# A two-layer decoder trunk on one core: raw transposes of the memory, new x's squares behind two high parts, interleaved attention heads, down's end by bank

## What is computed

```python
mem_n = rmsnorm(mem, mem_norm)                 # 256 memory tokens
for layer in range(2):
    h = rmsnorm(x, g[0])
    mix = even_mixer(h, ...) if layer % 2 == 0 else odd_mixer(h, ...)
    x = x + rmsnorm(mix, g[1])
    h = rmsnorm(x, g[2])
    x = x + rmsnorm(memory_cross_attention(h, mem_n, wq, wk, wv, wo), g[3])
    h = rmsnorm(x, g[4])
    x = x + rmsnorm((silu(h @ w_gate) * (h @ w_up)) @ w_down, g[5])
# memory_cross_attention: q = h @ wq, k = mem_n @ wk, v = mem_n @ wv, 4 heads of 512,
# p = softmax(q k^T / sqrt(512)), o = p v, o @ wo
```

## Time and profile before

| | before |
|---|---|
| median of 3 runs | 3000.12 us (2994.8 to 3000.22) |
| profiled execution, its own time | 2996.18 us |
| its span | 2994.4 us |
| mean granted TensorE clock | 0.984 of 2.4 GHz |
| VectorE busy | 2139.9 us (71%) |
| ScalarE busy | 1543.4 us (52%) |
| high part of a chunk, ScalarE, x550 | 1.914 us each |
| low part of a chunk, VectorE, x550 | 2.290 us each |
| squares of a token tile, ScalarE, x12 | 1.922 us each |
| `x_update`, VectorE, x10 | 2.346 us each |

### The profile page before, as it was taken

How to read it: one execution, slowest core, us unless ns; L and a number is a source line. 1 busy time by engine, 2 the same in 40 slices (tenths; PEclk the granted TensorE clock), 3 DMA queues, 4 the chain that set the end, 5 groups by cost and what they waited for, 6 DMA issues and landing times. The chain is left out here.

```text
span 2994.4 us, 31754 instructions
## 1 busy us (share of the span) xinstructions
PE 2890.6 (97%) x13082; PEld 2392.7 (80%) x13082; DVE 2139.9 (71%) x1443; ACT 1543.4 (52%) x1363; POOL 47.0 (2%) x97
## 2 busy tenths in 40 slices
PE   7999999999999999999998999999999999999998
PEld 6888788787787888887887877787787888887886
DVE  7888778568468988884456768567558888886454
ACT  5666556445345655664444445435435666555442
POOL 0000000000000000000000000000000000000000
PEclk9999999999999999999999989999999999999999
DMA  7664754655456455656554615644554655566552
GB/s 267 225 260 178 283 175 167 218 180 214 144 177 223 178 183 204 225 221 228 196 188 135 228 57 208 231 169 155 197 183 169 225 202 183 181 222 253 191 190 83
DMA packets 238272, 583.44 MB, mean 195 GB/s; under 512 B 8752, under 2 KB 8768, under 8 KB 222640
## 3 DMA queue, kind: packets, MB, share of 16 engines
q1 hardware_dynamic: 232896, 530.61, 49.8%
q0 software_dynamic: 4064, 38.21, 3.3%
q10 hardware_dynamic: 1168, 12.59, 1.0%
HBM read 564.60 MB, written 16.78 MB: 194 GB/s over the span
## 5 line engine op out<-in xcount | busy, mean ns | idle before, releaser
L1054 DVE TENSOR_TENSOR w_lo<-wide,w_hi 128x2048 fp32r<-128x2048 f32 x550 | 1250.9, 2290 | 490.9 <-ACT w_hi L554 487.8
L554 ACT ACTIVATE w_hi<-wide 128x2048 fp32r<-128x2048 f32 x550 | 1048.0, 1914 | 491.1 <-PE ps L1691 389.7
L1691 PE MATMUL ps<-w_hi,act_hi 128*128 128x512 f32 x3332 | 1227.8, 392 | 27.2 <-DVE w_lo L1054 11.5
L1691 PE MATMUL ps<-w_lo,act_hi 128*128 128x512 f32 x3332 | 1222.5, 391 | 0.0
L1691 PE MATMUL ps<-w_hi,act_lo 128*128 128x512 f32 x3332 | 1222.3, 391 | 0.0
L1691 PEld LDWEIGHTS ps<-w_hi,act_hi 128*128 128x128 f32 x3332 | 628.4, 189 | 163.1 <-issue 13.7
L1691 PEld LDWEIGHTS ps<-w_hi,act_lo 128*128 128x128 f32 x3332 | 628.8, 189 | 131.5
L1691 PEld LDWEIGHTS ps<-w_lo,act_hi 128*128 128x128 f32 x3332 | 629.1, 189 | 130.2 <-issue 0.2
L1058 DVE TENSOR_TENSOR wide<-wide,wide 128x2048 f32<-128x2048 f32 x105 | 240.5, 2290 | 4.8
L1691 PE MATMUL ps<-w_hi,s_hi_kept 128*128 128x512 f32 x368 | 149.0, 405 | 19.1 <-DVE nat L1615 13.6
L1009 ACT ACTIVATE act_hi<-mid 128x256 fp32r<-128x256 f32 x80 | 33.7, 421 | 240.4 <-PE ps L1691 240.4
(11 more groups left out here) (244 smaller groups left out, 1681.1 us busy)
## 6 DMA issues: line engine op xcount, KB each, us to landing
wide<-in_ffn_w_gate SPq DMA_DIRECT2D x88, 1024.0 KB, 7.7
wide<-in_ffn_w_up SPq DMA_DIRECT2D x88, 1024.0 KB, 7.1
wide<-in_ffn_w_down SPq DMA_DIRECT2D x88, 1024.0 KB, 4.9
wide<-in_odd_w_in SPq DMA_DIRECT2D x48, 1024.0 KB, 5.4
wide<-in_xattn_wk SPq DMA_DIRECT2D x32, 1024.0 KB, 8.2
wide<-in_xattn_wv SPq DMA_DIRECT2D x32, 1024.0 KB, 7.4
wide<-in_even_w_in SPq DMA_DIRECT2D x32, 1024.0 KB, 7.1
wide<-in_xattn_wq SPq DMA_DIRECT2D x32, 1024.0 KB, 5.2
```

What stands on the lines that cost most here:

```text
L554: nc.scalar.activation(w_hi[:, c % W_SLOTS, :], src, ACT.Copy).then_inc(hi_done, 2)
L1054: nc.vector.tensor_tensor(w_lo[:, c % W_SLOTS, :], src, w_hi[:, c % W_SLOTS, :].bitcast(F32), ALU.subtract).then_inc(lo_done, 2)
L1691: return nc.tensor.matmul(dst, lhs, rhs, start=start, stop=stop, skip_group_check=loose)
```

## The change

- The memory is transposed raw, its first half loaded in four quarters at the head of SP's queue, the second between chunks 1 and 2. The gain is the scale of the evacuations (`round_mem`, `rest_mem`), the root the scale of the keys' and values' evacuations. ScalarE's queue carries the vector rows first, now with `mem_norm`, and `x` after the second rounding. The squares of `x` lie in the second strip of the first keys, its `normed` in the value strips, its first transposes before the last product of the second layer's values.
- Behind a norm VectorE updates both halves of x at once, and takes the roots after the second low part and the first sums. ScalarE makes two high parts before it squares both halves.
- Attention goes head by head: scores, transposes and weighted values interleaved; the weighted values use banks 0 to 3; the next product waits for single banks.
- Down: the last `mid` transposes come before the fourth row; at the end one row is done for the first tile before the last three are waited for, one after another.

```diff
-    def stage(name, seven=(), rounds=0, rows=0, taken=True):
+    def stage(name, seven=(), rounds=0, rows=0, taken=True, uses=0):
...
+        at["u"] += uses
...
-        stage(f"x_pv{l}", rounds=2)
+        stage(f"x_pv{l}", uses=2)
...
-        return 4 + 4 * (TURNS.index(pre) + 1)
+        return 2 if pre == "mem_norm" else 4 + 4 * (TURNS.index(pre) + 1)
...
-        pxt = px
+        pxt = place("pxt", [XH, MT, T], F32, area + 16 * KB)
...
+        mem_in = [sem(f"mem_in{b}") for b in range(4)] + [sem("mem_in_other")]
+        pv_done = sem("pv_done")
...
+                if n == 2:
+                    sp.dma_start(memx[:, 1, :], mem[P:2 * P, :]).then_inc(mem_in[4], 16)
...
+            for b in range(4):
+                cols = slice(b * NB, (b + 1) * NB)
+                sp.dma_start(memx[:, 0, cols], mem[0:P, cols]).then_inc(mem_in[b], 16)
...
-            load_pre_gain(mem_norm)
-            load_gain(norms[0, 0])
...
+            roots([0, 1], rst_mem)
+            load_gain(norms[0, 0])
             roots([0, 1])
-            roots([0, 1])
-            pool.wait_ge(h_done, 4)
+            pool.wait_ge(h_done, 2)
...
-                pool.wait_ge(work_full[7], plan[f"x_pv{l}"]["rf"] + 2)
+                pool.wait_ge(pv_done, 8 * (l + 1))
...
-            for m in range(MT):
-                act.dma_start(memx[:, m, :], mem[m * P:(m + 1) * P, :]).then_inc(mem_in[m], 16)
+            act.dma_start(vec_rows[16:32, :], mem_norm.rearrange("(k p) -> k p", p=P)).then_inc(small_in, 16)
             act.dma_start(vec_rows[0:8, :], pool_scale.rearrange("(k p) -> k p", p=P)).then_inc(small_in, 16)
             act.dma_start(vec_rows[8:16, :], gate_b.rearrange("(k p) -> k p", p=P)).then_inc(small_in, 16)
-            act.dma_start(xres[:], x.rearrange("(m p) n -> p m n", p=P)).then_inc(x_in, 16)
 
...
+            def rest8(st, before_6=nothing, before_7=nothing):
                 split(st, 4)
-                before_5()
                 split(st, 5)
+                before_6()
...
-            def square_x(name, m, src=xres):
-
-                nc.scalar.activation(y[:, m, :], src[:, m, :], ACT.Square, accum_out=ssq[:, m:m + 1])\
+            def square_x(m, src=xres, junk=y):
+
+                nc.scalar.activation(junk[:, m, :], src[:, m, :], ACT.Square, accum_out=ssq[:, m:m + 1])\
                     .then_inc(sq_done, 1)
...
-                             (lambda: (take_t(0)(), take_t(1)())) if closes and i == 1 else take_t(0))
+                             take_t(0))
...
-                def new_x(m):
-                    xs_squared[0] += 1
-                    act.wait_ge(x_done, xs_squared[0])
-                    square_x(nxt, m)
-                new_x(0)
-                return lambda: new_x(1)
+                def new_x():
+                    for m in range(MT):
+                        xs_squared[0] += 1
+                        act.wait_ge(x_done, xs_squared[0])
+                        square_x(m)
+                return new_x
...
+            def round_mem(m):
+
+
+                act.wait_ge(vec_done, 1)
+                for b in range(4):
+                    act.wait_ge(work_full[WORK + b], plan["mem_norm"]["rf"] + m + 1)
+                    for k in range(4):
+                        t = 4 * b + k
+                        ins = nc.scalar.activation(act_hi[:, t, m * P:(m + 1) * P], ps[:, WORK + b, k * P:(k + 1) * P],
+                                                   ACT.Copy, scale=vec[:, 16 + t:17 + t])
+                    ins.then_inc(hi_ev, 1)
...
-            act.wait_ge(mem_in[0], 16)
-            square_x("mem_norm", 0, memx)
-            split_halves(first, 0)
-            act.wait_ge(mem_in[1], 16)
-            square_x("mem_norm", 1, memx)
-            round_transposes("mem_norm", 0)
-            split_halves(first, 1)
-            split_halves(first, 2)
-            split_halves(first, 3)
-            round_transposes("mem_norm", 1)
-            act.wait_ge(x_in, 16)
+            round_mem(0)
+            for s in range(4):
+                split_halves(first, s)
+            round_mem(1)
+            act.dma_start(y[:], x.rearrange("(m p) n -> p m n", p=P)).then_inc(x_in, 16)
             for m in range(MT):
-                square_x("pre_mix0", m)
+                square_x(m, memx, hx)
+
+            def x_squares():
+                act.wait_ge(x_in, 16)
+                for m in range(MT):
+                    square_x(m, y, hx)
...
-                take_k = transposed(f"mk{l}", kx, mv[0])
+                take_k = transposed(f"mk{l}", kx, mv[0], second=x_squares if l == 0 else nothing,
+                                    scale=rst_mem, pre="mem_norm")
...
-                natural(mv[0], vx, 0, mv[1], take_k)
-                natural(mv[1], vx, 2 * NB, strip_of("mk1" if l == 0 else "sb_qk"), store_k)
+                natural(mv[0], vx, 0, mv[1], take_k, scale=rst_mem)
+                natural(mv[1], vx, 2 * NB, strip_of("mk1" if l == 0 else "sb_qk"), store_k, scale=rst_mem)
...
-                transposed(f"xq{l}", qx, strip_of(f"x_out{l}"), late, closes=True)
+                take_q = transposed(f"xq{l}", qx, strip_of(f"x_out{l}"), late)
 
                 act.wait_ge(xs_ready, 2 * (l + 1))
+
+                def take_pt(h):
+                    act.wait_ge(work_full[WORK + h], plan[f"x_pt{l}"]["rf"] + 1)
+                    nc.scalar.activation(pxt[:, h, :, :], ps[:, WORK + h, :].rearrange("p (k t) -> p k t", t=T), ACT.Copy)\
+                        .then_inc(bank_free[WORK + h], 1)
                 for h in range(XH):
+                    if h == 1:
+                        take_q()
+                    if h == 3:
+                        take_pt(0)
...
+                take_pt(2)
+                for g in range(8):
+                    act.wait_ge(pv_done, 8 * l + g + 1)
+                    nc.scalar.activation(act_hi[:, 2 * g:2 * g + 2, :], ps[:, g % 4, :].rearrange("p (k t) -> p k t", t=T),
+                                         ACT.Copy).then_inc(hi_ev, 1)
...
-                        rest8(st, before_5, other_sums, first_sums)
+                        rest8(st, nothing, other_sums, lambda: (first_sums(), before_6()))
...
-                                                   take_t(0)(), take_t(1)() if closes and i == 1 else None))
+                                                   take_t(0)()))
...
                 x_update(0)
-
                 xs_done[0] += 2
-                x_0 = xs_done[0] - 1
+                dve.wait_ge(x_done, xs_done[0] - 1)
+                x_update(1)
 
                 def late():
-                    dve.wait_ge(x_done, x_0)
-                    x_update(1)
                     x_root(0)
                     x_root(1)
...
+            def rest_mem(m):
+
+                e0 = hi_ev_at["mem_norm"]
+                for b in range(4):
+                    dve.wait_ge(hi_ev, e0 + 4 * m + b + 1)
+                    for k in range(4):
+                        t, tok = 4 * b + k, slice(m * P, (m + 1) * P)
+                        ins = nc.vector.scalar_tensor_tensor(
+                            out=act_lo[:, t, tok], in0=ps[:, WORK + b, k * P:(k + 1) * P], scalar=vec[:, 16 + t:17 + t],
+                            in1=act_hi[:, t, tok].bitcast(F32), op0=ALU.mult, op1=ALU.subtract)
+                    ins.then_inc(bank_free[WORK + b], 1)
+            rest_mem(0)
+            for s in range(4):
+                split(first, s, (0, 1))
+            rest_mem(1)
+
...
+            def x_roots():
+                for m in range(MT):
+                    x_root(m)
+
+            def x_normed(m):
+                def run():
+                    if m == 0:
+                        gain_ready()
+                        root_ready()
+                    normed(m, y, gain)
+                return run
...
-                take_k = transposed(f"mk{l}", kx, mv[0])
+                if l == 0:
+                    for m in range(MT):
+                        x_root(m)
+                take_k = transposed(f"mk{l}", kx, mv[0], second=x_roots if l == 0 else nothing,
+                                    scale=rst_mem)
...
+                natural(mv[0], vx, 0, mv[1], take_k, nothing if l else x_normed(0), scale=rst_mem)
+                natural(mv[1], vx, 2 * NB, strip_of("mk1" if l == 0 else "sb_qk"), nothing,
+                        nothing if l else x_normed(1), scale=rst_mem)
...
+                largest(0)
+                take_q()
+                shares(0)
+                largest(1)
+                shares(1)
+                largest(2)
+                take_pt(1)
+                shares(2)
+                largest(3)
+                shares(3)
+                take_pt(3)
+                rest_tiles(f"x_pv{l}", [k % 4 for k in range(8)], 0)
...
-                rest8(gu[0], late, other_sums, first_sums)
+                rest8(gu[0], nothing, other_sums, lambda: (first_sums(), late()))
...
+                    if ready is not None:
```

(78 more changed lines are left out.)

127 lines of the change are left out of this document (36 added, 91 removed).

## The result

The changed kernel takes **2926.8 us** (median of 4 runs, 2925.4 to 2928.2) against 2998.5 us for the kernel before on the same chip: a ratio of 0.976, 95% interval 0.975 to 0.978. The profiled execution took 2927.3 us, its span 2925.6, so the span is 68.8 us shorter; the forecast was 72.2 us shorter, and 2926 us for the median.

A forecast was written before the change was run, and what follows sets the result against it. TensorE, busy 97% of the span, was taken as the bound, leaving its waits and half-clock time to win. Terms summed to -72.2 us from 2996.2, so 2924.0, forecast as 2926 us for the median; range 2906 to 2959.

The forecast's parts named there:

- gate/up: Gate/up strip, both layers: 6.8 us waits shrink to 2.1 without a clock fall, -15.6 us (-9.4 if falls stay).
- gated projection: Gated linear projection: first wait goes with its short fall, second becomes 3.6 us behind x's spill; net -3.6 us (0 to -8).
- attention: Attention in both layers: interleaving heads puts 16 matmuls in front of each TensorE wait, -16.0 us (-11 to -18).
- Opening: Kernel start: vector rows and memory's first half load first, so the first weight product comes earlier, -10.0 us (-6 to -13).
- x's squares in the key strip: First key strip: two squares ahead of ScalarE's copy and split make product 5 late, +1.6 us (0 to +3.9).
- x's transposes: Before the first layer's projection: wait grows to 5.1-5.3 us, plus half a long fall, +3.5 us (+1.9 to +3.5).
- Query projections: Both layers' query projections: waits of 0.43 and 4.00 us go, with one short and one long fall, -13.5 us.
- rival 1: Clock falls stay although waits shrink: nine falls counted as gone, 23 us, giving 2949 us; chance 0.08.
- Down's end: End of down, both layers: 4.90 us wait shrinks to 0.8 without a fall, -14.4 us (-8.2 with falls).
- `mid`: `mid` transposes one row earlier: 12 matmuls cover the 1.2 us copy, twice, -2.4 us (0 if VectorE is late).
- 3 and 4: Third: summed strips become VectorE-bound, could eat all 72 us, chance 0.03. Fourth: edits don't act, 2994 to 3006, chance 0.02.
- Rival 2: Stall behind each norm moves to later summed products; five heads give 10 instead of 33 us, 2949 us; chance 0.17.

The follow-up runs named there:

- Experiment 10: Changed kernel with a small early ScalarE activation before the memory arrives and x's squares ahead of a split: 2926.0 us.
- experiment 8: Changed kernel with x's first transposes back behind the last product of the second layer's values: 2928.5 us.
- experiment 9: Changed kernel with the first three banks of x's transposes emptied by both engines ahead of the last split before them: 2921.6 us.
- experiment 2: Changed kernel with ScalarE's old order of x's squares, first ahead of the second quad's first high part, second behind it: 2945.0 us.
- experiment 3: As experiment 2, plus VectorE making the four other token sums directly behind the variances, ahead of the next low part: 2932.7 us.
- experiment 4: Changed kernel with GpSimd issuing the copy of x between the two pairs of roots, ahead of the gate's weight loads: 2917.7 us.
- experiment 7: Changed kernel with TensorE's attention by stage and VectorE's and ScalarE's copies of the turned shares behind all four heads: 2931.8 us.
- experiment 5: Changed kernel with down's end as before, all four last rows waited for together, then bank by bank: 2940.7 us.
- experiment 12: Changed kernel with the edits of experiment 4, experiment 9 and Experiment 10, plus the token sums' order of experiment 3: 2906.6 us.

## Why the prediction was right, point by point

The time came out at 2926.8 for 2926. That is better than its terms and in part luck: gate/up was off by 4.8 us and the gated projection by 2.9, attention by 2.5 the other way, the rest by less than 2 each. Together the terms were 3.4 us too hopeful (68.8 for 72.2). The profiled execution was 2927.3, so 3.3 above the 2924.0 of the sum; the median lies 0.5 below it, where I had added 1.95.

- **Opening (-8.8 for -10).** The evacuations were faster than forecast: 16 in 4.23 us, one every 0.25 us, where I took 0.30. The transposes began at 6.4 us instead of 5.5. What the sum left out is the table load of 1.28 us. In the kernel before it stood in the first 5 us, under the loads, because ScalarE had squares to make; with the squares of `mem` gone the first activation is the evacuation itself. Removing work removed the cover of something that hung on it. Experiment 10 shows the 1.3 us. `x` loaded behind the weights cost nothing, as said.
- **x's squares in the key strip (+1.6 for +1.6)**: a wait of 1.3 us.
- **x's transposes (+1.7 for +3.5).** The wait is 5.13 us as forecast. The half fall charged on top didn't come: before, the clock is 0.51 over the 3.4 us behind this wait, and after it is 0.52, so only the 1.7 us of waiting are paid. Experiments 8 and 9 bear out the mechanism and its place. They also show that 1.7 us there aren't measurable in the total.
- **Query projections (-13.5 for -13.5)**: all four waits gone, and the falls with them. The model (a head without late squares) held. The single prices did not: the falls were worth 1.9 and 2.7 us for 1.55 and 3.1. The window of the earlier trace rows that shows 0.50 for the second layer begins at 2090.40 us, 1.7 us before the end of its wait (2092.14); taken from there on, the same length reads 0.63:

```profile
2092.10:2098.90 6.80, 6.76 (x24) 5.78 (x25) 6.33 (x4) 5.07 (x6) 0.00 (x0) 0.63 0.00 0
```

- **Gate/up (-10.8 for -15.6) is the term that was mis-sized.** The waits did what they should: 6.83 and 6.79 to 2.35, for a forecast of 2.1. The price of the falls was wrong. I counted 3.1 us for each, but before, the clock fell *inside* the wait. Windows of the kernel before (columns as in rows 4), around the end of that wait at 943.45 us:

```profile
940.00:943.40 3.40, 0.00 (x0) 0.00 (x0) 3.40 (x4) 3.40 (x4) 0.00 (x0) 0.51 0.00 0
943.40:946.80 3.40, 3.35 (x8) 2.68 (x9) 3.40 (x3) 1.04 (x1) 0.00 (x0) 0.50 0.02 5
```

  Of 6.8 us at the low level one half passed while TensorE stood anyway; only 3.4 us of work ran slow, which costs 1.7. And in the second layer a fall remained behind the 2.35 us wait; the kernel after, from that wait's end:

```profile
2258.73:2262.50 3.77, 3.77 (x10) 2.95 (x11) 3.77 (x3) 0.99 (x1) 0.00 (x0) 0.55 0.00 0
```

  So 4.5 + 1.7 and 4.4 + 0.2 were won. The summed strips behind lost nothing: the one wait there, for `p_sb`, is 1.1 us in both kernels and both layers. This is rival 1 in a small part: one fall of nine stayed.
- **Gated projection (-0.7 for -3.6).** The working itself gives 3.2 and not 3.6 (2.86 + 1.55 gained, 1.2 lost). The second wait, by the copy of x, was forecast at 3.6 and is 4.7 us: the copy took 9.6 us instead of 8.1, and it left 0.9 us later, behind the held power. The first, forecast to go, is 1.1 us: the second power was held for 2.27 us by the low part beside it. In the kernel before the powers at that place took 0.55 us each. Experiments 2 to 4 show both.
- **Attention (-18.5 for -16.0).** 29.9 us in the first layer and 31.0 in the second, against 31.1 forecast for each: TensorE doesn't wait at all in the first layer, 0.85 us in the second. I had kept back 1.3 us for small waits, which weren't there, and set the first layer's work 1.2 us too high. My account of the cause was wrong in its weight: I put it all on the heads' interleaving on TensorE, and that is 2.0 us in a layer (experiment 7); the rest came with the other parts of the same edit.
- **Down's end (-14.2 for -14.4)** and **`mid` (-3.0 for -2.4)**: the former as worked out, with 0.63 us left of 4.90; undoing it gives 12.7 of the 14.2 us back (experiment 5). For the latter I counted the wait alone; 0.6 us more went with it.
- **The marks.** Idle time was forecast near 50 us; it is 56.2 (2925.6 less 2869.4), for 103.8 before. "No falls behind the short waits" was wrong once.
- **Rivals.** 3 and 4 are excluded by the result. Rival 2 (the stall moves) came true only at the gated projection, where the second wait grew from 2.40 to 4.70 us while the first shrank from 2.86 to 1.12; 1.2 us of that was in the forecast. Of rival 1's nine falls one stayed, worth 1.6 us by experiment 4.

## What to carry to other kernels

A small operation of GpSimd that others wait for shouldn't be issued just behind a long VectorE instruction with two SBUF operands. Put short ones there where the wait is real (12 us in experiment 3, nothing in experiment 12), and put the transfers that gate the next stage ahead of other work in that queue (9 us here for this one issue, moved at three places). When you price a clock fall, look at how much of the low stretch lies in the wait itself; only what lies behind it costs. When you take work away from the start of an engine, ask what else it was paying for there, such as the table load.

## What the runs showed of the hardware that I had not expected

- **A one-column power takes 0.55 us, or up to 2.6 us**, by what VectorE began just before it. In the kernel after, one of the ten powers of the five projections was held, 2.27 us; in experiment 2 the first of every pair was, 2.59 us. In the opening of the kernel before one took 1.46 us beside a low part of half a chunk (1.22 us) and again ended 0.41 us behind it. At gate/up of the kernel after the second power began 0.11 us before the low part and took 0.55 us.
- **The same gap doesn't always end in the same fall.** Waits of 2.35 us at gate/up left the clock at 1.00 in the first layer and 0.55 in the second. Gains of 1 to 2 us at one place were also taken back or kept elsewhere (experiments 8, 9, 10 and 12): an edit worth under 2 us can't be judged by the total alone.
- **The granted clock of the windows isn't to be read before the first long work.** They show 1.00 for the sixteen transposes of the opening. A window of the kernel after, and two of the kernel before:

```profile
6.39:8.00 1.61, 1.61 (x8) 1.61 (x9) 0.00 (x0) 0.44 (x1) 0.00 (x0) 1.00 0.95 351
...
24.30:28.70 4.40, 4.37 (x10) 3.47 (x11) 4.40 (x7) 4.38 (x6) 1.46 (x1) 1.00 1.05 387
28.70:33.10 4.40, 4.40 (x20) 3.49 (x19) 4.40 (x4) 2.20 (x3) 0.00 (x0) 1.00 1.05 387
```

  But the transposes run 0.21 us apart (16 in 3.56 us), while eight of the same shape take 1.03 us later on the earlier trace rows, and the first products of the kernel before run at half the pace of the next ones (10 and 20 in 4.40 us) under the same 1.00. The pace is that of the low level; the window's column isn't.
